# A diffusion block's first mixer rebuilt as two blocks, its projections in three passes of float32r, and a router that works on four tiles at once

## The reference, cut to what matters

```python
def diff_attention(hx, hy, w_qkv, w_o, q_g, k_g, lq1, lk1, lq2, lk2, sub_g, lambda_init, cos, sin, ...):
    lam = exp(sum(lq1 * lk1)) - exp(sum(lq2 * lk2)) + lambda_init
    q, k, v = split_qkv(hx, w_qkv)                  # h @ w_qkv
    q = apply_axial_rope(rms_norm(q, q_g), cos, sin)
    k = apply_axial_rope(rms_norm(k, k_g), cos, sin)
    qy, ky, vy = split_qkv(hy, w_qkv)
    ky = rms_norm(ky, k_g)
    keys, vals = concatenate([ky, k]), concatenate([vy, v])
    s = q . keys / sqrt(64)                         # per head, per half c
    p = softmax(s);  a = p[:, :, 0] - lam * p[:, :, 1];  o = a @ vals
    return (rms_norm(o, sub_g) * (1.0 - lambda_init)) @ w_o

def apply_axial_rope(t, cos, sin):                  # pairs of 16-wide groups
    out = stack([t1 * cs - t2 * sn, t2 * cs + t1 * sn])

def hier_moe(h, w_group, b_group, w_expert, b_expert, ...):
    grp = argmax(h @ w_group + b_group)             # one of 4 groups
    top_v, top_i = top_k((h @ w_expert + b_expert)[grp], 2)   # 2 of its 8 experts
    weight = softmax(g_logits)[grp] * softmax(top_v)
```

## Time and profile before

| | before |
|---|---|
| median of three runs | 3614.17 us (3613.68 to 3619.74) |
| profiled execution, its own time | 3620.49 us |
| its span | 3618.7 us |
| TensorE, share of the span | 3192.8 us, 88% |
| VectorE / ScalarE / GpSimd | 1413.9 (39%) / 875.3 (24%) / 118.6 (3%) |
| mean granted TensorE clock | 0.942 |
| first mixer, norm to the last residual (665.9 to 1229.4) | 563.5 us |
| its norm / Q, K, V / attention / output | 33.9 / 273.9 / 166.6 / 89.1 us |

### The profile page before, as it was taken

The page is one execution under the profiler, slowest core; times in us unless marked ns, Lnnn a source line. Parts: engine busy times, 40 slices in busy tenths (PEclk is TensorE's granted clock), DMA queues, the critical chain, the costliest instruction groups (busy, mean ns, idle before and its releaser), DMA issues. The chain is left out here.

```text
span 3618.7 us, 35945 instructions
## 1 busy us (share of the span) xinstructions
PE 3192.8 (88%) x13732; PEld 2272.5 (63%) x13732; DVE 1413.9 (39%) x2158; ACT 875.3 (24%) x1405; POOL 118.6 (3%) x118
## 2 busy tenths in 40 slices
PE   2999999799888899999999899999896788959995
PEld 1888888446743387877888447888685465343332
DVE  6546454355164264644333204333321563131113
ACT  2211111311253122224322204222331353011111
POOL 0000000010000000000000000000000100002220
PEclk9999999899998999999999999999998788969997
DMA  4422322110100265532222112222222000327883
GB/s 169 155 90 111 127 82 114 59 47 35 47 1 0 83 230 184 226 132 83 95 102 93 41 41 87 96 102 83 85 99 102 1 0 12 139 105 301 336 352 132
DMA packets 78692, 395.88 MB, mean 109 GB/s; under 512 B 17280, under 2 KB 18688, under 8 KB 52608
## 3 DMA queue, kind: packets, MB, share of 16 engines
q1 hardware_dynamic: 67072, 386.10, 28.7%
q0 software_dynamic: 11520, 8.43, 0.8%
HBM read 444.80 MB, written 16.78 MB: 128 GB/s over the span
## 5 line engine op out<-in xcount | busy, mean ns | idle before, releaser
L555 PE MATMUL ps<-h_high_ffn,weights_high_ffn 128*128 128x512 f32 (+1 forms) x1696 | 624.9, 368 | 16.7 <-DVE weights_low_ffn L675 12.9
L556 PE MATMUL ps<-h_low_ffn,weights_high_ffn 128*128 128x512 f32 (+1 forms) x1696 | 624.2, 368 | 0.0
L557 PE MATMUL ps<-h_high_ffn,weights_low_ffn 128*128 128x512 f32 (+1 forms) x1696 | 623.7, 368 | 0.0
L632 ACT ACTIVATE weights_high_ffn<-weights 128x2048 fp32r<-128x2048 f32 (+4 forms) x168 | 259.5, 1544 | 473.3 <-PE ps L557 395.6
L555 PEld LDWEIGHTS ps<-h_high_ffn,weights_high_ffn 128*128 128x128 f32 x1696 | 320.8, 189 | 71.6 <-DVE weights_low_ffn L675 14.1
L675 DVE TENSOR_TENSOR weights_low_ffn<-weights,weights_high_ffn 128x2048 fp32r<-128x2048 f32 (+4 forms) x168 | 308.0, 1833 | 147.0 <-ACT weights_high_ffn L632 144.6
L556 PEld LDWEIGHTS ps<-h_low_ffn,weights_high_ffn 128*128 128x128 f32 x1696 | 320.7, 189 | 52.8
L557 PEld LDWEIGHTS ps<-h_high_ffn,weights_low_ffn 128*128 128x128 f32 x1696 | 320.4, 189 | 53.1
L555 PE MATMUL ps<-hidden_high_ffn,weights_high_ffn 128*128 128x512 f32 (+1 forms) x880 | 326.5, 371 | 17.7 <-DVE weights_low_ffn L675 10.4
L556 PE MATMUL ps<-hidden_low_ffn,weights_high_ffn 128*128 128x512 f32 (+1 forms) x880 | 325.1, 369 | 0.0
L557 PE MATMUL ps<-hidden_high_ffn,weights_low_ffn 128*128 128x512 f32 (+1 forms) x880 | 325.1, 369 | 0.0
(11 more groups left out here) (310 smaller groups left out, 3924.2 us busy)
## 6 DMA issues: line engine op xcount, KB each, us to landing
weights<-in_ffn_gu SPq DMA_DIRECT2D x88, 1024.0 KB, 4.8
big<-in_w_exp_gu SPq DMA_DIRECT2D x32, 2048.0 KB, 13.3
scratch_ffn<-in_w_mod SPq DMA_DIRECT2D x35, 1536.0 KB, 6.5
weights<-in_ffn_d SPq DMA_DIRECT2D x24, 768.0 KB, 4.2
weights<-in_w_in SPq DMA_DIRECT2D x16, 1024.0 KB, 4.8
weights<-in_ffn_d SPq DMA_DIRECT2D x24, 640.0 KB, 3.9
weights<-in_w_exp_dn SPq DMA_DIRECT2D x15, 1024.0 KB, 14.1
hbuf<-in_w_exp_dn SPq DMA_DIRECT2D x12, 1024.0 KB, 16.1
```

The costliest lines, as they stand in the source:

```text
L555: pe.matmul(out, wh, xh, start=(k == 0), stop=False)
L556: pe.matmul(out, wh, xl, start=False, stop=False)
L557: mm = pe.matmul(out, wl, xh, start=False, stop=(k == n - 1))
L632: scalar.activation(w_high[:, s, 0:n], ring.buf[:, s, 0:n], ACT.Copy).then_inc(high_done[s].sem, 1)
```

## The change

The four stages of the mixer between two feed-forwards become one function, `first_mixer`, with two blocks: norm, Q, K and V in the first, attention, output norm and output projection in the second. In detail:
- **Projections in three passes.** Q, K, V and the output projection now use high and low parts like the feed-forwards. ScalarE and VectorE make 16 pairs of head weights of 1024 columns, four slabs for V and four for the output, and the two parts of the normed input and output.
- **The start.** Tables are made ahead of the norm. ScalarE runs one root on a dummy first, so that its table is loaded early. The norm works on x first and the context later, and the first three heads of Q are computed side by side, one k at a time, as the input's k tiles get ready.
- **One root for all heads.** For each head two windows of a small matrix (`pick`) put its square sums into two of 16 rows, summed over all heads in one PSUM bank; one root and one reciprocal on 16 rows follow for Q, and one for K. TensorE then spreads two rows of them back over 128 partitions (`spread`), each row to 64 partitions, before each head is finished.
- **Rotation by shuffle.** VectorE swaps groups of 16 partitions (`stream_shuffle`), in place of the product with `rot`.
- **Loops unrolled.** All of it is written out, and K's heads are finished during V.
- **Attention.** The same order, with the head's output in one bank (6) in place of two; its squares (ScalarE) and their sums (`out_sums`, bank 7) come during the turns. The split of the output's first weight slab lies in turns 1 and 2.
- **Output.** The first slab's two tiles are interleaved by k, behind the spreading products.
- **Router.** Steps for four tiles become one instruction each, with broadcast operands.

```diff
+        def spread(pe, bank, n, hd, rows):
+
+            for c in range(2):
+                mm = pe.matmul(ps[c * HD:(c + 1) * HD, bank, 0:n], ident[0:HB, 2 * hd + c:2 * hd + c + 1].to_broadcast([HB, HD]),
+                               rows, start=True, stop=True)
+            return mm
...
+                def three(out, i, k, a, n, stop):
+                    wh, wl = (w[:, k * P:(k + 1) * P] for w in split[home_of[i]])
+                    pe.matmul(out, wh, h_high[:, k, a:a + n], start=(k == 0), stop=False)
+                    pe.matmul(out, wh, h_low[:, k, a:a + n], start=False, stop=False)
+                    return pe.matmul(out, wl, h_high[:, k, a:a + n], start=False, stop=stop)
+
+                def square_sums(i):
+                    pe.wait_ge(fm["evacuated"].sem, i + 1)
+                    hd = i % HEADS
+                    first, last = hd == 0, hd == HEADS - 1
+                    if i < HEADS:
+                        mm = pe.matmul(ps[0:HB, 6, :], window(hd), sq[:, i % 2, 0:NX], start=first, stop=last)
+                    else:
+                        pe.matmul(ps[0:HB, 4, :], window(hd), sq[:, i % 2, 0:NX], start=first, stop=last)
+                        mm = pe.matmul(ps[0:HB, 5, 0:NY], window(hd), sq[:, i % 2, NX:NT], start=first, stop=last)
+                    mm.then_inc(fm["head_summed"].sem, 1)
+
+                def turn_head(i):
+
+                    hd, which = i % HEADS, i // HEADS
+                    pe.wait_ge(fm["rows_ready"].sem, 1 + which)
+                    if i > 0:
+                        pe.wait_ge(fm["head_ready"].sem, i)
+                    T, rows = (Q, rows_q) if which == 0 else (K, rows_k)
+                    mm = spread(pe, 7, NX, hd, rows[0:HB, 0:NX])
+                    if which:
+                        mm = spread(pe, 5, NY, hd, rows[0:HB, NX:NT])
+                    mm.then_inc(fm["head_turned"].sem, 1)
...
+                    weights(i)
+                for k in range(KD):
+                    pe.wait_ge(fm["in_low"].sem, k + 1)
+                    for i in range(3):
...
+                    for c, (a, n) in enumerate(STREAMS):
+                        for k in range(KD):
+                            mm = three(ps[:, 2 * (t % 2) + c, 0:n], i, k, a, n, k == KD - 1)
+                    mm.then_inc(fm["product"].sem, 1)
+                    while done < i:
+                        square_sums(done)
+                        done += 1
+                    if t > 0:
...
+                        pe.matmul(out, h_high[:, k, tok], v_high[v % 2][:, k, :], start=(k == 0), stop=False)
+                        pe.matmul(out, h_high[:, k, tok], v_low[v % 2][:, k, :], start=False, stop=False)
+                        mm = pe.matmul(out, h_low[:, k, tok], v_high[v % 2][:, k, :], start=False, stop=(k == KD - 1))
...
+                    if z == 0:
+                        square_sums(done)
+                        turn_head(HEADS - 1)
+                    if z in BK:
+                        turn_head(HEADS + BK[z])
...
+                    for k in range(KD + 1):
+                        if k < KD:
+                            scale_in(k, c)
+                        if k > 0:
+                            in_low(k - 1, c)
+                        if k in between:
+                            w_low(between[k])
+
+                def finish_head(i):
+                    hd, which = i % HEADS, i // HEADS
+                    T = (Q, K)[which]
+                    vector.wait_ge(fm["evacuated"].sem, i + 1)
+                    if i > 0:
+                        vector.wait_ge(fm["head_ready"].sem, i)
+                    hstep_(vector.stream_shuffle(part, T[:, hd, 0:NX], SWAP))
+                    vector.wait_ge(fm["head_turned"].sem, i + 1)
+                    if which:
+                        hstep_(vector.scalar_tensor_tensor(K[:, hd, NX:NT], K[:, hd, NX:NT], qkg[:, 1:2], ps[:, 5, 0:NY],
+                                                           ALU.mult, ALU.mult))
+                    hdone()
+                    vector.sem_inc(fm["head_swapped"].sem, 1)
+                    hstep_(vector.tensor_tensor(part, part, sines[:, which, :], ALU.mult))
+                    hdone()
+                    vector.wait_ge(fm["head_cos"].sem, i + 1)
+                    hstep_(vector.tensor_tensor(part, part, T[:, hd, 0:NX], ALU.add))
+                    hdone()
+                    vector.tensor_tensor(T[:, hd, 0:NX], part, ps[:, 7, :], ALU.mult).then_inc(fm["head_ready"].sem, 1)
+
...
+                def out_sums(hd):
+                    pe.wait_ge(fm["out_squared"].sem, hd + 1)
+                    pe.matmul(ps[0:HEADS, 7, :], pick_one(hd), sqo[:, hd % 2, :], start=(hd == 0), stop=False)\
+                        .then_inc(fm["out_summed"].sem, 1)
...
+                    if u >= 2 * QT and u % QT == 1:
+                        out_sums(u // QT - 2)
...
+                pe.wait_ge(fm["out_root"].sem, 2)
+                for j in range(HEADS):
+                    if j >= 3:
+                        pe.wait_ge(fm["out_normed"].sem, j - 2)
+                    pe.matmul(ps[:, j % 3, :], ident[0:HEADS, j:j + 1].to_broadcast([HEADS, P]), rstd[0:HEADS, 0:NX],
+                              start=True, stop=True).then_inc(fm["out_spread"].sem, 1)
...
-                    each(lambda i: vector.scalar_tensor_tensor(eq[:, i, 0:n], src(i), m(i), rev[:, NE - n:NE],
-                                                               ALU.is_ge, ALU.mult))
-                    each(lambda i: vector.reduce_max(t2(i), eq[:, i, 0:n], AX_X))
-                    each(lambda i: vector.tensor_scalar(dst(i), eq[:, i, 0:n], t2(i), None, ALU.is_ge))
+                    one(vector.tensor_tensor(eq[:, :, 0:n], src, over(m, n), ALU.is_ge))
+                    one(vector.tensor_tensor(eq[:, :, 0:n], eq[:, :, 0:n], rows(rev[:, NE - n:NE], n), ALU.mult))
+                    one(vector.reduce_max(t2, eq[:, :, 0:n], AX_X))
...
-                each(lambda i: vector.scalar_tensor_tensor(row[:, i, :], nearer[:, i, :], CAP - 0.5, shift,
-                                                           ALU.is_ge, ALU.mult))
-                each(lambda i: vector.tensor_tensor(row[:, i, :], row[:, i, :], nearer[:, i, :], ALU.add))
-                each(lambda i: vector.tensor_tensor(row[:, i, :], row[:, i, :], base, ALU.add))
+                one(vector.scalar_tensor_tensor(row, nearer, CAP - 0.5, rows(shift, NE), ALU.is_ge, ALU.mult))
+                one(vector.tensor_tensor(row, row, nearer, ALU.add))
+                one(vector.tensor_tensor(row, row, rows(base, NE), ALU.add))
...
-    own = stage_buffers("_0")
-    with nc.Block() as block:
-        norm(block, NT, mod_gain[0][:, 1], chunk(0, 3))
-        attention_tables(block)
...
-    with nc.Block() as block:
-        head_inputs(block, 0, Qh, two(io["w_qk"], 4))
-        head_inputs(block, 1, Kh, two(io["w_v"]))
-        values(block, Vh, two(io["w_o"]))
-    attention(Qh, Kh, Vh, Oh)
-    with nc.Block() as block:
-        output_norm(block, Oh, subg[:, 1:2])
-        project_residual(block, io["w_o"], Oh, chunk(0, 5), first_gu("ffn2", 0), [scaled])
-    own.close()
+    first_mixer(first_gu("ffn2", 0))
```

810 lines of the change are left out of this document (473 added, 337 removed).

## The result

The changed kernel takes 3527.9 us (median of 4 runs, 3527.7 to 3529.9) beside 3616.95 for the kernel before on the same chip: a ratio of 0.9755 with a 95% interval of 0.9738 to 0.9771, 89 us less. Forecast were 3535, with a range of 3515 to 3575. On another occasion it took 3525.1 (5 runs, ratio 0.9748, 0.9735 to 0.9762). The two profiled executions differ by 90.6 us (3620.49 and 3529.9), forecast 79.2.

What follows compares the result with a forecast made beforehand. PE's own work was taken to bound the Q, K, V stage, and chains over engines the rest. Start -9.5, Q, K, V -46.9, attention +4.5, output -21.0 and router -6.3 sum to -79.2: 3535 us, range 3515 to 3575.

Steps and rivals of the forecast that it cites:

- Three passes: Projections: three passes in place of plain float32 products take Q, K, V from 220.7 to 179.2 us, output 55.0 to 43.5.
- Small products: First block: square sums and spreads on PE, 32 groups with 0.25 us added to each, cost 42.4 us.
- What must hide behind PE: First block: VectorE's head chains (3.8 us, K 4.3) and ScalarE's work stay hidden; 0, bounds 0 and +8 us.
- rival 1: First block: VectorE becomes the bound, with a slow shuffle and GpSimd's product drawn out; +15 us, 3550; chance 0.10.
- The start: From the mixer's norm to the first projection: first product at 690.3 in place of 699.8, -9.5 us, bounds -12 and -6.
- Attention: First mixer's attention: output sums add 3.6 us and the split of a weight slab 0.9; +4.5, bounds -2 and +8.
- Output: Output norm and projection: shorter way to the spreads, same spreads, three-pass projection of 46.6 us; -21.0, bounds -24 and -16.
- Router: Router, logits to assignments: 11.9 us become 6.0, three more steps behind the counts save 0.5; -6.3, bounds -7 and -3.
- 2: First block: the halves of a spread don't overlap; +17 us, 3552; chance 0.12 together with the attention rival, 3.
- 5: Projections: three passes bring nothing, since static code or three operands run slower than in the loops; 3588 us; chance 0.03.
- 3: Attention grows more than said by sums and splits, eating the output's gain; +12 us, 3547; chance 0.12 together with 2.
- 4: First block: small groups on few rows pull PE's clock down, slower than before; 3647 us at half the work; chance 0.03.

Runs made afterwards that it cites:

- plain_qkv: The changed kernel with Q, K and V projected by one plain float32 product in place of three passes, products with low parts left out: 3567.0 us.
- spreads_more: The changed kernel with each K spread of the first block done four times more for its 512 columns: 3575.7 us.
- vector_longer: The changed kernel with five more VectorE operations of 128x512 in each of the 16 heads' chains in the first block: 3548.1 us.

## Why the prediction was right, point by point

- **As a whole.** The forecast of 3535 was 7 us too high, and by the medians the change is worth 89 us, give or take 6. By the stretches, with the second trace of the first mixer of before, it is worth about 85 and not 79.2: 3.4 more in the router, 1.5 in the output, 1.0 in attention, 0.7 in the first block, and 0.7 less at the start. The terms are right one by one, so the total owes little to luck.
- **Three passes, -53 with the output.** Right in mechanism and size for Q, K and V (`plain_qkv`: 39 to 42 us, 41.6 by my counts). The output's 11.5 have no run of their own; they are read from its projection, 47.1 us for 46.6 forecast.
- **Small products.** I gave 42.4 us to the 32 groups. They take 38.1 (0.96 a Q sum, 2.40 a K sum with a Q spread, 1.43 a K spread), and 4.1 us show in the full products beside them, since each group of these is some 0.22 longer than its passes alone (8.55 for 8.32). The 0.25 that I added for a change of shape was there, but stood on the other side, in the full products behind the group. The Trainium skill (TensorEngine Tiling, Key Properties) has a drain at a change of tiling mode. Whether these 0.22 us are that drain, no run tells: the spread in one piece, without the halves, took no less (1.05 for 1.00).
- **What must hide behind PE.** Hidden, as forecast. The shuffle at 0.73 is at my lower bound; the sine product was wrong by 1.1 us, which rival 1 had named as its condition, and took 1.1 of the 3.0 us a K head that I had left free (7.3 - 4.3): 1.9 remain. ScalarE's work grew less than I said, to 58.6 us and not 85, at no cost.
- **The start, -9.5.** -10.2 measured. The roots, the first product and the clock's cold start are within 0.7 us.
- **Attention, +4.5.** The term of the sums was right (3.6 forecast, 3.9 measured). That of the split (0.9) is open: up to the first copy the stage grew by 0.4 against one trace of before and by 2.3 against the other. Left out of the sum was the clock: 2.9 us at the last product with V, which not every trace shows.
- **Output, -21.0.** -20.7: copy to first spread 7.4 (7.9), spreads 13.95 (13.6), projection with the last residual 47.1 (46.6).
- **Router, -6.3.** The step from logits to assignments was right (6.0). The mis-sized term is what stands behind it: I priced three steps of VectorE at 0.5 and no change on PE, and it was 3.8, 2.9 of it in the counts at 1.00 of the clock in place of 0.50.
- **What is no effect.** The 1.4 us of the next feed-forward's norm and the 4.1 of the second mixer belong to the profiled execution of before.
- **The range.** The two terms that I named for its lower end, 8 us of the first block and 6.5 of attention, lead from 3535 to 3520.5 and not to 3517.
- **Rivals.** 1, 2 and 5 are excluded by an experiment each, 3 by the trace. 4 is excluded for this kernel, and shown to be near: pieces of 4.9 us brought it about (`spreads_more`).

Open is what in the first attention moves the clock from one kernel to another (167.0 to 172.4 us with the same code); no run was made for it.

## What to carry to other kernels

Where one engine is busy nine tenths of a stage, count its instructions by the spacing in the rows and let the rest go, but measure what slack the hidden chain has: here 2 us a head kept a product that ran 2.5 times as long as its shape says. Shortening a chain of another engine can pay twice, as in the router, where PE's next work came nearer to its last and met the full clock; and a stall can cost twice, as in `vector_longer`, where 13.6 us of waits brought 11.0 us of slower products. One trace of each kernel is not enough for differences of 1 to 4 us; a second trace of the same code tells what they are worth. A long run of products on few rows is best padded with zeros to the full height, or broken up between full products.

## What the runs showed of the hardware

- A run of products on 8 of 128 rows doesn't hold TensorE's clock, though the engine is busy throughout: 0.50 through 16 spreads in a row, a fall in mid-run where they began at 1.00, and a rise to 1.00 in mid-run once the same spreads have 128 rows. The time goes from 13.95 to 9.4 us, with idle products ahead to 7.1. On 16 rows, pieces of 4.9 us took the V stretch from 1.00 to 0.77.
- Waits of up to 2.9 us between full products lowered the clock of a stretch from 0.99 to 0.94 (`vector_longer`), and the same products took 235.5 us for 224.4.
- The same code met different clocks in different executions: at the first norm's sums 11.58 or 13.28 us from squares to roots, at the end of attention 0.66 to 1.00.
- Products on full rows that nothing reads keep the clock up over a stall (1.00 from 668.3 to 702.3).
- A VectorE product of two SBUF operands, 128x512, takes 692 ns alone and 1760 beside GpSimd's of the same kind; GpSimd's takes 1.3 us.
- VectorE's swap of partition groups (`stream_shuffle`) on 128x512 float32 takes 0.73 us, hardly more than a copy (0.69).
- Two float32 products on 64 columns each, one on either half of the output partitions, take together what one on 128 columns takes, even as pairs on 16 rows (a spread 1.00 in halves and 1.05 in one piece; with a K sum 2.40 and 2.44).
